# A hybrid decoder step on one core: the decay rates' products spread over three feature tiles

## The reference, cut to what matters

```python
p = hn @ w_in
qkv, z, b, a, c_q, c_kv, k_pe = split_cols(p, IN_SIZES)
...
beta = jax.nn.sigmoid(b)
g = -jnp.exp(a_log) * jax.nn.softplus(a + dt_bias)
...
g = jnp.cumsum(g, axis=-1)                      # within a chunk
decay = jnp.where(lower, jnp.exp(g[..., :, None] - g[..., None, :]), 0.0)
lmat = jnp.where(strict, jnp.einsum('bnhid,bnhjd->bnhij', k_beta, k) * decay, 0.0)
amat = lmat + jnp.eye(chunk)
sol = lax.linalg.triangular_solve(amat, rhs, ...)   # u and w of each chunk
qk = jnp.where(lower, jnp.einsum('bnhid,bnhjd->bnhij', q, k) * decay, 0.0)
...
v_new = u_c - w_c @ s                            # the recurrence over chunks
s = s * jnp.exp(gl) + k_dec.T @ v_new
```

## Time and profile before

| | us |
|---|---|
| median of 3 runs (1024.67 to 1026.63) | 1024.68 |
| time of the profiled execution | 1028.57 |
| its span | 1026.7 |
| PE busy | 979.0 |
| DVE busy | 513.3 |
| ACT busy | 446.5 |
| POOL busy | 157.4 |

### The profile page before, as it was taken

How to read it: one execution, slowest core, us unless ns; L and a number is a source line. 1 busy time by engine, 2 the same in 40 slices (tenths; PEclk the granted TensorE clock), 3 DMA queues, 4 the chain that set the end, 5 groups by cost and what they waited for, 6 DMA issues and landing times.

```text
span 1026.7 us, 20657 instructions
## 1 busy us (share of the span) xinstructions
PE 979.0 (95%) x8604; PEld 848.7 (83%) x8604; DVE 513.3 (50%) x980; ACT 446.5 (43%) x964; POOL 157.4 (15%) x257
## 2 busy tenths in 40 slices
PE   4999999999989989899999999999999999999997
PEld 3988899877757556566666899999999999999996
DVE  5655766665476385354545533543343344334433
ACT  5545638566636676344445423421231134113312
POOL 1020500255520300255452000000000000000000
PEclk9999969999999999899999999999999999999999
DMA  7312111120024600477773321422232222222202
GB/s 248 107 61 83 43 42 41 47 65 10 3 58 105 227 2 4 182 247 243 250 254 116 124 83 41 145 82 83 98 109 83 82 83 83 82 87 103 99 1 87
DMA packets 31655, 102.58 MB, mean 100 GB/s; under 512 B 14023, under 2 KB 14967, under 8 KB 25218
## 3 DMA queue, kind: packets, MB, share of 16 engines
q1 hardware_dynamic: 22346, 63.50, 18.8%
q0 software_dynamic: 9216, 37.75, 10.7%
HBM read 96.45 MB, written 4.22 MB: 98 GB/s over the span
## 4 chain that ended last, share of the span: by engine, by line
PE 88%; DVE 6%; ACT 3%; issue 2%; DMA 1%; SPq 0%; DVEq 0%; ACTq 0%
PE PS L597 17%; PE PS L599 17%; PE PS L598 17%; PE PS L1086 7%; PE PS L1097 3%; PE PS L1123 3%; PE PS L732 2%; PE PS L1106 1%; PE PS L805 1%; PE PS L836 1%; PE PS L888 1%; DMA RAW<-in_w_stream 1%; PE PS L987 1%; PE PS L579 1%; DVE SMX L2183 1%
## 5 line engine op out<-in xcount | busy, mean ns | idle before, releaser
L597 PE MATMUL PS<-XH,WH 128*128 128x272 f32 (+1 forms) x896 | 261.2, 292 | 0.0
L599 PE MATMUL PS<-XH,WL 128*128 128x272 f32 (+1 forms) x896 | 260.6, 291 | 0.0
L598 PE MATMUL PS<-XL,WH 128*128 128x272 f32 (+1 forms) x896 | 259.7, 290 | 0.0
L1250 ACT ACTIVATE WH<-RAW 128x2048 fp32r<-128x2048 f32 x46 | 88.0, 1914 | 196.0 <-PE PS L599 191.8
L597 PEld LDWEIGHTS PS<-XH,WH 128*128 128x128 f32 x896 | 169.2, 189 | 4.8 <-issue 4.2
L598 PEld LDWEIGHTS PS<-XL,WH 128*128 128x128 f32 x896 | 169.4, 189 | 0.0
L599 PEld LDWEIGHTS PS<-XH,WL 128*128 128x128 f32 x896 | 169.3, 189 | 0.0
L597 PE MATMUL PS<-NH,WH 128*128 128x272 f32 x512 | 149.1, 291 | 0.8 <-DVE WL L1766 0.8
L599 PE MATMUL PS<-NH,WL 128*128 128x272 f32 x512 | 147.6, 288 | 0.0
L598 PE MATMUL PS<-NL,WH 128*128 128x272 f32 x512 | 146.6, 286 | 0.0
L1766 DVE TENSOR_TENSOR WL<-RAW,WH 128x2048 fp32r<-128x2048 f32 (+2 forms) x51 | 108.6, 2129 | 66.7 <-ACT WH L1250 64.8
(11 more groups left out here) (336 smaller groups left out, 1543.1 us busy)
## 6 DMA issues: line engine op xcount, KB each, us to landing
RAW<-in_w_stream SPq DMA_DIRECT2D x47, 1024.0 KB, 4.9
XN<-in_hin SPq DMA_DIRECT2D x4, 512.0 KB, 6.7
out_y_p<-YO SPq DMA_DIRECT2D x4, 512.0 KB, 2.7
CST<-in_big SPq DMA_DIRECT2D x1, 1132.5 KB, 13.8
SS<-in_sstate SPq DMA_DIRECT2D x1, 1024.0 KB, 5.1
out_ssm_s<-SS SPq DMA_DIRECT2D x4, 256.0 KB
CN<-in_cache,IDX POOLq DMA_INDIRECT x64
WQN<-in_wq SPq DMA_DIRECT2D x3, 256.0 KB, 5.9
```

The costliest lines, as they stand in the source:

```text
L597: pe.matmul(PS[:, b, 0:n], wh, xh[:, k, c:c + n], start=(k == 0), stop=False)
L598: pe.matmul(PS[:, b, 0:n], wh, xl[:, k, c:c + n], start=False, stop=False)
L599: last = pe.matmul(PS[:, b, 0:n], wl, xh[:, k, c:c + n], start=False, stop=(k == DT - 1))
L1250: act.activation(WH[w % 2][:, :, :], RAW[w % 2][:, :, :], ACT.Copy).then_inc(sem("w_high"), 1)
```

## The change

The 16 rate products are no longer one block. One is issued ahead of each contraction step: t = 0 to 5 at steps 2 to 7 of tile 13, 6 to 13 at the steps of tile 14, 14 and 15 at steps 0 and 1 of tile 15. Spread 1 goes by halves to steps 2 and 5 of tile 14, spread 2 to steps 5 and 6 of tile 15. The pairs go to steps 1 to 4 of tile 15, in bank 4 and no longer 5. The chunk transposes move from behind tile 14 to behind tile 15. The first 24 gate products move from behind the solved transposes to ahead of them. ACT does the rates, exponentials and last rates behind the copy of tile 14, the chunk copies behind that of tile 15, silu_out(10) behind that of tile 13, silu_out(11) after the last rates, and the root of the query latent's norm ahead of the copy of tile 18. DVE does both last convolutions and weights_low(8) ahead of the rates, behind the first column product and both masks.

```diff
+            def spread_half(x, half):
+
+                if x and half == 0:
                     pe.wait_ge(sem("col_used"), x)
+                    pe.wait_ge(sem("qk_inverted"), 2)
+                (c, n), b = HALVES[half], 6 + half
+                last = pe.matmul(PS[:, b, 0:n], row("hexp"), BROW[:, (3, 1, 4)[x], c:c + n], start=True, stop=True)
+                if half == 1:
+                    last.then_inc(sem("col_spread"), 1)
+
+            def gate_column(t):
+
+                if t == 0:
+                    pe.wait_ge(sem("e16_in"), 16)
+                    pe.wait_ge(sem("dve_step"), DVE_STEP["gates"])
+                    pe.wait_ge(sem("qk_inverted"), 2)
+                    pe.wait_ge(sem("kk_copied"), 2)
+                last = pe.matmul(PS[:, 5, 0:5 * NU], row("e16", t), BROW[:, :, t:T:CH], start=(t == 0), stop=(t == CH - 1))
+                if t == CH - 1:
+                    last.then_inc(sem("pe_step"), 1)
+
+            def gate_pair(p):
+
+                if p == 0:
+                    pe.wait_ge(sem("kk_copied"), 3)
+                pe.matmul(PS[:, 4, 192 + NU * p:192 + NU * p + NU], row("bpair", p), BROW[:, 1, CH - 1:T:CH],
+                          start=True, stop=True)
+                pe.matmul(PS[:, 4, 352 + BS * p:352 + BS * p + BS], row("bpair", p), BROW[:, 1, NP + TS - 1:T:TS],
+                          start=True, stop=True)
+
+            def among_13(k):
+
+                if k >= 2:
+                    gate_column(k - 2)
+
+            def among_14(k):
+
+                gate_column(6 + k)
+                if k in (2, 5):
+                    spread_half(1, k // 4)
+
+            def among_15(k):
+
+                if k < 2:
+                    gate_column(14 + k)
+                elif k >= 5:
+                    if k < 7:
+                        spread_half(2, k - 5)
+                if 1 <= k < 5:
+                    gate_pair(k - 1)
...
-                    last = weight_tile(i // 2, i % 2, (XH, XL), (b, b + 1), HALVES)
+                    last = weight_tile(i // 2, i % 2, (XH, XL), (b, b + 1), HALVES,
+                                       {13: among_13, 14: among_14, 15: among_15}.get(i))
...
                 if i == 11:
-                    spread_rows(0)
-                elif i == 12:
-                    gates_to_columns()
-                    spread_rows(1)
-                elif i == 13:
-                    spread_rows(2)
-                elif i == 14:
+                    first_spread()
+                elif i == 15:
                     for x in range(4):
                         chunk_transposes(x)
...
                     sum_squares("cq", 3)
+                    gate_products(range(0, 3 * DT))
                     solved_transposes(0)
                     solved_transposes(1)
...
-            gate_products(range(0, 3 * DT + 6))
+            gate_products(range(3 * DT, 3 * DT + 6))
...
                     else:
+                        act.wait_ge(sem("lat_done"), 2)
+                        root("cq", 3, QL)
                         dst, f = ZG[:, m - 18, :], ACT.Silu
...
-                if i and TILES[i - 1] < 12:
+                if 1 <= i < 13 and TILES[i - 1] < 12:
                     silu_out(CONV.index(TILES[i - 1]))
...
+                elif i == 13:
+                    silu_out(10)
+                elif i == 14:
                     rates()
-                elif i == 13:
                     act.wait_ge(sem("dve_step"), DVE_STEP["decay_diff"])
                     act.activation(TMP[:, :, :], TMP[:, :, :], ACT.Exp, scale=-1.0).then_inc(sem("act_step"), 1)
                     last_rates()
-                elif i == 14:
+                    silu_out(11)
+                elif i == 15:
                     act.wait_ge(sem("silu_done"), 12)
                     for x in range(4):
                         copy_chunks(x)
...
                     by_column(KK, 0)
+                    masked(KK, "m_lower")
+                    link(masked(KQ, "m_updiag"))
+                    convolve(10, TILES[12])
+                    convolve(11, TILES[13])
+                    weights_low(8)
                     rate_products()
-                    link(masked(KK, "m_lower"))
                     decay_differences()
-                    masked(KQ, "m_updiag")
                     link(scaled(KK, 10))
                     link(scaled(KQ, 3))
+                    key_matrix()
+                    by_column(KQ, 2)
+                    query_matrix()
                     rate_exponents()
-                elif i == 13:
-                    key_matrix()
-                    query_matrix()
```

More of the change, by code:

```diff
@@ L556, in head_sums @@
                 last.then_inc(sem("qk_summed"), 1)
[L558 to L564, removed]
-                    pe.wait_ge(sem("col_used"), x)
[L566 to L585, removed]
+            def first_spread():
+                pe.wait_ge(sem("rows_in"), 16)
+                pe.wait_ge(sem("qk_root"), 2)
+                pe.wait_ge(sem("qk_inverted"), 1)
+                spread_half(0, 0)
+                spread_half(0, 1)
@@ L1348, in last_rates @@
                 act.wait_ge(sem("col_spread"), 3)
-                act.activation(EGL[:, :, :], PS[:, 5, 192:192 + PAIRS * NU].rearrange("p (x u) -> p x u", x=PAIRS), ACT.Exp)
-                act.activation(EGLS[:, :, :], PS[:, 5, 352:352 + PAIRS * BS].rearrange("p (x u) -> p x u", x=PAIRS),
+                act.activation(EGL[:, :, :], PS[:, 4, 192:192 + PAIRS * NU].rearrange("p (x u) -> p x u", x=PAIRS), ACT.Exp)
+                act.activation(EGLS[:, :, :], PS[:, 4, 352:352 + PAIRS * BS].rearrange("p (x u) -> p x u", x=PAIRS),
                                ACT.Exp).then_inc(sem("act_step"), 1)
@@ L1498, in _ @@
                         copy_chunks(x)
-                elif i == 15:
                     act.wait_ge(sem("p_copied"), 16)
@@ L1512, in _ @@
                 elif i == 18:
-                    act.wait_ge(sem("lat_done"), 2)
-                    root("cq", 3, QL)
                     gate_out(0)
@@ L1920, in query_matrix @@
             def query_matrix():
-                by_column(KQ, 2)
+                dve.wait_ge(sem("conv_done"), 11)
                 dve.tensor_tensor(AT[:, :, :], KQ[:, :, :], decays[1], ALU.mult).then_inc(sem("at_done"), 1)
@@ L1958, in _ @@
             for i, m in enumerate(TILES[:EARLY]):
-                if i % 2 == 0 and i < 16:
+                if i % 2 == 0 and i < 14:
                     weights_low(i // 2 + 1)
-                if m < 12:
+                if m < 12 and i < 12:
                     convolve(CONV.index(m), m)
```

## The result

The changed kernel takes 1036.57 us (median of 4 runs, 1032.57 to 1043.52), against 1025.23 us for the kernel before on the same chip (4 runs, 1024.67 to 1026.63). The ratio is 1.0116, interval 1.0094 to 1.0138: 11 us slower. The forecast was 1025.5, range 1020.0 to 1030.5; it was added to 1024.68, the median of the first three runs of the kernel before. The profiled execution took 1036.71 us with a span of 1034.9.

A forecast was written before the change was run, and what follows sets the result against it. TensorE, busy 979.0 of 1026.7 us, was taken as the bound. Terms of -0.8 (front), +0.5, +0.95 and 0.15 us gave +0.8 on the median 1024.68, so 1025.5 us, range 1020.0 to 1030.5.

The forecast's parts named there:

- (2): Tiles 13 to 15: full clock throughout, gaining 4.6 us on tile 13, spread and pairs; the rate products gain nothing.
- the sum: Terms from the end of tile 12 to the start of tile 16: 41.1 us against 41.9 before.
- a rival at 0.11: Clock falls all the same in tiles 13 to 15: steps 2.7 us, 6 lose 1.0 each, 1031.5 us; chance 0.11.
- (1): Wait before the first rate product: tile 13's steps 0 and 1 run in it, gain 1.5 us.
- (3): Boundaries between dense 128-row and 8-row products: 21 islands at 0.33 or 0.375 us each, loss 7.2 us.
- (4): Stall before the chunk transposes: no wait there in the new order, transposes near 164 us, gain 1.2 us.
- (5): ACT's queue behind the last spread: PE's sums wait for LATT copy, chunk copies and squares, loss 0.5 us.
- (6): VectorE's substitution before the solved transposes: PE arrives about 1 us after they are ready, no loss.
- (7): 24 gate products moved ahead of the solved transposes no longer cover what follows them: loss 0.95 us.
- rival of hidden boundaries: Island boundaries cost 0 to 0.2 us each: 1018.3 us with none, 1022.5 with 0.2; chance 0.18.
- late chain: ACT behind silu_out(11), or the inverse at the solved transposes, comes late: +2 us, 1027.7 us; chance 0.13.

The follow-up runs named there:

- a_contig: The changed kernel with its 16 rate products reading 35 neighbouring columns instead of every 16th (wrong rate values): 1018.04 us, ratio 0.9989 to the kernel before.
- a_128rows: The changed kernel with each rate product replaced by one of 128 rows of other data, same column step of 16: 1019.53 us, ratio 1.0012.
- a_gates_back: The changed kernel with the 24 gate products again behind the solved transposes and the root behind the copy of tile 18: 1037.91 us, ratio 1.0115.
- a_pairs_of_two: The changed kernel with two rate products ahead of every other step in place of one at each: 1033.41 us, ratio 1.0075.
- a_block: The changed kernel with all 16 rate products in one block at step 2 of tile 13: 1023.03 us, ratio 1.0040.
- b_gates_first: The kernel before with only the 24 gate products moved ahead of the solved transposes and the root ahead of tile 18's copy: 1022.92 us, ratio 1.0043.
- p_after: The changed kernel with rate, spread and pair operands zero-padded to 128 partitions and rate products reading neighbouring columns, right values: 1013.47 us, ratio 0.9939.
- p_before: The kernel before with operands zero-padded to 128 partitions and neighbouring columns, rate products still one block behind tile 12: 1019.26 us, ratio 0.9998.
- p_gates_back: p_after with the 24 gate products again behind the solved transposes: 1015.28 us, ratio 0.9954.
- the second group: a_pairs_of_two, a_gates_back, b_contig and a repeat of the kernel before, run on one chip beside the kernel before at 1025.68 us.
- b_contig: The kernel before, its block of rate products reading neighbouring columns instead of every 16th (wrong rate values): 1024.66 us, ratio 0.9993.

## Why the prediction was wrong

The step that failed is (2), the clock: "I take full clock", from the recurrence's 1.00. The clock went to 0.50 at 146 us, after 21 us of steps of 1.73 us, and stayed for 27. Measured from the end of tile 12 to tile 16, the changed kernel takes 52.1 us where the sum says 41.1. Of these 11.0, 0.04 x 16 = 0.6 is the boundary taken too small, and the rest, some 10.4, is half clock (10.9 by the front of a_contig). That it is the clock, and that the islands' make brings it down, is shown: a_contig and a_128rows keep order, places and count of the products, change one thing in each, and both hold 1.00 there, while a_gates_back repeats the stretch of 27.3 us. Which side of the make does it is not shown: either change also shortens the step, to 1.47 and 1.36 us from 1.73, and no run kept the step's length with other products in it.

The same cause stood as a rival at 0.11, named for tiles 13 to 15 (tile 13 kept 1.00; the fall came in tile 14), with the right step (2.7 us; measured 2.57 with a rate product and 2.65 with a pair). Its price was too low: it let the stretch last 17 us as before and reckoned 6 steps. It lasted 27, to the transposes, 10 to 11 steps and the transposes' start lay in it, at about 1.0 us each: 10.4 and not 6. The range ended at 1030.5, below even this rival's own 1031.5.

What should have warned is in the rows ahead of the prediction. I compared the new steps with the recurrence by dense work (8 products in 3 us). But the earlier trace rows has 220 products in 15 us, 14.7 per us; the new steps start 8 in 1.73 us, 4.6 per us, and the block in which the clock fell before 3.4 (one each 0.297 us). By count the recurrence was the less like of the two rows, and the block the more like. This says which row to compare with, and is no law of the clock: a_pairs_of_two starts 16 in 3.1 us and loses it.

The other steps:
- (1) Wait, gain 1.5: right. Left over are 0.44 us.
- (2) "The rates give nothing at full clock": right, 0.59 us at 1.00 in a_128rows, and in a_block 9.70 us for the block, as before.
- (3) Boundaries: right at full clock. 0.36 per island against 0.33 (1.73 less 0.77 and 0.59). At half clock it is 0.60 (2.57 less 0.59 and six dense products of 0.23). a_128rows shows them gone with equal rows. The Trainium skill ("TensorE: Matmul & The Clock Gate", Architectural detail) has loads pulled ahead of running matmuls; the trace agrees for 128 rows beside 128 and disagrees for 8.
- (4) No wait before the transposes: right, though they come 8.6 us later than the forecast's 164, and 10.8 later if both are counted from the first rate product, for the clock.
- (5) Loss 0.5 before L534: none in the changed kernel, as PE was slower than ACT; 0.6 in a_contig, where it was not. The chain was right, and its wait hung on step (2). The drain that the Trainium skill ("ScalarE: Activation LUTs", What ACT_TABLE_LOAD costs) adds is not seen here either: silu_out(11)'s load stands at 170.10 with 1.28 us, its activation at 171.39.
- (6) The solved transposes without a wait: right (202.74, no wait).
- (7) Loss 0.95: right for the part alone (1.0 to 1.3 in b_gates_first), and the path too: 3.65 us from L688 to L736 and 6.74 to the recurrence, where 3.6 and 6.7 were forecast. In company the part is worth nothing (a_gates_back), and the tail's 1.1 us would have come without it.

The rival of hidden boundaries fell. The late chain is real (1.8 us in a_gates_back) but covered by the moved gate products.

What stays open: what brings the further short stretches at half clock, outside the front, and what each costs. They differ from run to run. They go with a gap that the runs show and the traces don't explain. In the two groups whose kernel before has a mean clock of 0.989, each variant is 2 to 4 us worse against it as a whole than from the first rate product to the recurrence: a_contig (3.1 better there, 1.1 as a whole), a_128rows, a_block, b_gates_first (1.0 worse, then 4.4), p_after (10.4 better, then 6.2), p_before, p_gates_back. In the second group, and for the changed kernel itself, the gap is -1.1 to +0.6 us. Span x (1 - clock) x 2 is the time at half clock, if all that is missing is at 0.50. By it p_after's median run has 12 us and the kernel before beside it 22, 10 less, although the 17 us of the front are gone: so p_after has some 7 us more elsewhere (its trace has stretches of 3.4 us at about 291 and 332 us that the kernel before's lacks). That would be worth some 3 us by the relation below, which is an estimate; no trace of the kernel before at 0.989 was kept to show it.

Over the four runs of the changed kernel this time is 31, 41, 46 and 56 us for times of 1032.57, 1036.43, 1036.71 and 1043.52: about 0.43 us per us. The spread of its runs, 11 us against 2 before, goes with it.

## What to carry to other kernels

Filling PE's gaps can cost more than the gaps: before taking full clock for the filled stretch, find the row that is most like it in shape and count of products, and if the clock fell there, carry half clock as a case with the whole stretch's price, since PE's busy share (100% in both) won't tell. Products scattered among dense ones should have the dense ones' row count (padded with zeros) and read neighbouring columns; either kept the clock here in the new order, and both together turned +1.2% into -0.6%. In the old order they bought nothing (b_contig 0.9993, p_before 0.9998). A loss worked out for one part alone (0.95 us) need not be its own in the company of the others: work out the waits behind a moved part with and without it, for the whole change.

## What the runs showed of the hardware

- The clock can fall without a gap in PE's work: 21 us of gapless steps at 1.00 and then 0.50 for 27 us, until 3.5 us behind the last island (the changed kernel, and again a_gates_back).
- An fp32 product over 175 columns with a step of 16 elements takes 0.297 us per instruction with 8 rows, at 1.00 and at 0.50, and with 128 rows at 1.00. With neighbouring columns it is about 0.15 at 1.00 (p_after) and 0.29 at 0.50 (b_contig), so that the step costs time at full clock only.
- An 8-row stationary among 128-row ones costs 0.36 us per island with strided columns at 1.00 and 0.60 at 0.50 (a step of 2.57 less 0.59 and six dense products of 0.23), and about as much with neighbours: 1.47 less 0.77, and less the 0.31 that the pair takes in p_after, leaves 0.39. With 128 rows it costs nothing (a_128rows).
- Padding a contraction with 120 rows of zeros cost nothing that PE's timeline shows (0.47 us for the pair of 175 columns with their pipelined end, where it is 0.57 with 8 rows).
